# The last unit of a MoE encoder: adding the residual in the output banks with TensorE, and the last chunk's products ahead of the scatters

## The chip, the cores and the metric

One core of a Trainium2 chip runs the whole kernel. The metric is the device time of one execution in microseconds (us), as the median of several runs.

## What is computed

One encoder layer on 256 tokens of width 1024, all in fp32: a mixer with attention in two head groups, and then the part that matters here, a mixture of experts, followed by the last norm:

```python
h = h + mix @ w_o[l]
h = h + hier_moe(rms_norm(h, norm2_g[l]), ...)      # 32 experts, top-2 of one group of 8
return rms_norm(h, final_g)
# an expert: (silu(x @ w_gate) * (x @ w_up) * combine) @ w_down,  w_gate and w_up 1024x512, w_down 512x1024
```

Every expert's weights (6 MB) are read from HBM, 32 experts, so about 200 MB in all. At the end stands h plus the experts' sum, normalised by the root of its mean square and multiplied with final_g.

## The kernel before

The program is written by hand, engine by engine, with semaphores; nothing is scheduled for it. The tokens lie in two tiles of 128 (t = 0, 1), and each tile's 1024 columns in two halves of 512. The columns of h are kept permuted: the tile holds 8 blocks of 128 columns (`h_cols`, each block contiguous), and `h_rows` is the same memory read so that 8 elements in succession lie 128 elements (512 bytes) apart.

```python
h_cols = h.rearrange("p t (c k) -> p t c k", c=KC)
h_rows = h.rearrange("p t (c k) -> p t k c", c=KC)
```

The experts are worked through in ten units (`UNITS`) of two or four experts (`WAYS`); the last three have four. A unit gathers its tokens (L1266), multiplies with gate and up (`products`, L1304), takes silu times up on DVE (L963), transposes that on TensorE (`turn_act`, L1316), copies it back to SBUF on DVE (`hT_out`, L958), multiplies with down (`down_chunk`, L1322), copies the result out on ACT (`down_out`, L670, into `y_slots`) and scatters it onto the tokens with one matmul per tile and half (`scatter`, L1355). The scatters of all units accumulate in the four banks Y0 to Y3 (bank Y0 + 2t + half), which stay open through the whole mixture. Unit i's scatter is issued two units later, behind the gate products; in the last unit, i = 9, both scatter(7) and scatter(8) stand between the gate and the up products.

Weights come through a ring of 12 slots of 2 MB, issued by SP in the order of use; each load waits until the products that used the slot are done. The last unit's down weights come in four pieces (`LAST_PIECES`, L427): chunks 0 and 1, chunk 2, the first half of chunk 3, its second half. TensorE multiplies them as they land (`last_products(0)` to `(3)`), with the spreading of final_g over the partitions between them (L1448, eight matmuls, copied out by ACT, L668). `last_scatter(k)` (L1442) adds one tile and half in the order `LAST_ORDER` = (0,0), (1,0), (0,1), (1,1).

After each of the four last scatters DVE adds h to the bank into `h_sum` in SBUF (L1026), reading `h_rows`. ACT squares each sum with an accumulator (L694). POOL multiplies tile 0's first half with final_g (L523), DVE tile 1's (L1058). DVE adds the two sums of squares of a tile (L1057, L1060), POOL raises to the power -0.5 (L526), DVE scales the second halves (L1063) and ACT the first (L699), and three DMAs write the output (L443, L445, L701).

A float32 matmul stands in the trace as two passes, each with its own load of the stationary operand, and four experts of 32 rows each run side by side in the array: 16 such matmuls are 32 rows of the trace, in 8 groups of four.

Of the kernel before, what the change touches and what calls it, by code (L numbers as in the profile page):

```python
# [10 lines left out]
ALU = mybir.AluOpType  # L11
# [4 lines left out]
D = 1024  # L16
# [101 lines left out]
def build_encoder(nc, x, x_cols, gain_cols, norm1_g, w_in, qn_g, kn_g, sink, rel_bias, gnorm_a, gnorm_b, w_o, norm2_g,  # L118
# [11 lines left out]
    with ExitStack() as ctx:  # L130
# [108 lines left out]
        def scratch(n):  # L239
# [52 lines left out]
            sem, ("down_done", "y_ready", "place_ready", "scattered", "summed"))  # L292
        ov_turned, ov_nT, ov_free, ov_in, ov_gu, ov_silu, ov_act, ov_act_turned, ov_hT, ov_y, ov_added = map(
# [155 lines left out]
        def _(pool):  # L449
# [71 lines left out]
            pool.wait_ge(final_g_cut, 1)  # L521
            pool.wait_ge(ssf_ready, 1)
            pool.tensor_tensor(final_out[:, 0, 0:512], h_sum[:, 0, 0:512], final_gb[:, 0:512], ALU.mult).then_inc(gained_t0, 1)  # L523
# [5 lines left out]
        def _(act):  # L529
# [154 lines left out]
            with act.If(over > 0):  # L684
# [4 lines left out]
                act.wait_ge(ov_added, TT * EXPERTS)  # L689
# [14 lines left out]
        def _(dve):  # L704
# [319 lines left out]
            for k, (t, half) in enumerate(LAST_ORDER):  # L1024
                dve.wait_ge(scattered, 4 * UNITS + k + 1)
                dve.tensor_tensor(h_sum[:, t, 512 * half:512 * half + 512].rearrange("p (k c) -> p k c", c=KC), h_rows[:, t, 64 * half:64 * half + 64, :],  # L1026
                                  ps[Y0 + 2 * t + half][:].rearrange("p (k c) -> p k c", c=KC), ALU.add).then_inc(summed, 1)

            over = dve.value_load(over_flag[0:1, 0:1], min_val=0, max_val=1)
            with dve.If(over > 0):  # L1030
                ov_nT_sb = slots[3].rearrange("p (c t) -> p c t", c=16)
                link(dve.tensor_tensor(weight_over, weight_over, bcast(rstd2, 2, EXPERTS), ALU.mult))
# [496 lines left out]
```

## Time and profile before

| what | value |
|---|---|
| median of 3 runs | 568.03 us (567.9 to 568.98) |
| the profiled execution, its own time | 568.0 us |
| span from first to last instruction in it | 565.7 us, so 2.3 us lie around it |
| PE busy, DVE busy, ACT busy | 80%, 20%, 12% of the span |
| DMA | 217.67 MB at a mean of 385 GB/s |
| mean granted TensorE clock | 0.904 of full speed |

The profile has a page with shares of busy time, a chain of work followed back from the last instruction, and groups of instructions. The trace behind it gives single instructions in order of time: start, duration, engine, line of the kernel, operation, output and inputs, how often in a row, and in brackets how long the engine had been idle before it and what ended that. `x8` after a matmul counts passes.

### The profile page before, as it was taken

Reading aid. Unit: us, or ns where it says so; the run is one execution under the profiler, and the core shown is the slowest. Engines: PE = TensorE matmul, PEld = TensorE weight load, DVE = VectorE, ACT = ScalarE, POOL = GpSimd, SP = SyncE. Lnnn points to the kernel's source line nnn. Section 1 sums busy time; section 2 is a strip of 40 time slices with the busy share of each in tenths; the row PEclk is TensorE's granted clock in tenths of the full one; section 3 lists DMA queues with packets and bytes.
Section 4 is the critical chain, followed back from the end, with each engine's and each line's share of the span. In section 5 each row is a group of like instructions: output and inputs, shape, how many; then the busy total and the mean of one; then the engine's idle time right before and its main releaser. Section 6 shows DMA issues by size and latency. Waiting matters only on the chain.

```text
span 565.7 us, 6390 instructions
## 1 busy us (share of the span) xinstructions
PE 452.3 (80%) x2562; PEld 204.1 (36%) x2562; DVE 111.4 (20%) x353; ACT 67.9 (12%) x160; POOL 23.6 (4%) x53
## 2 busy tenths in 40 slices
PE   9999999989999996478999936952776385557884
PEld 3456776474535342132353401410223021312231
DVE  1017764262112030030110300300021001200004
ACT  1125332121010100100101001000100000000104
POOL 0232200100000000000000000000000000000001
PEclk9999999999999998797999968877977787876988
DMA  8989991947999999999999999999999999999981
GB/s 305 382 333 429 425 367 29 416 151 232 410 392 422 428 426 425 429 431 427 423 426 430 430 426 427 426 426 426 426 432 432 425 427 426 426 426 427 423 342 76
DMA packets 27390, 217.67 MB, mean 385 GB/s; under 512 B 5433, under 2 KB 6713, under 8 KB 14561
## 3 DMA queue, kind: packets, MB, share of 16 engines
q1 hardware_dynamic: 23120, 215.09, 91.5%
q10 hardware_dynamic: 4240, 2.17, 1.4%
q8 instruction: 21, 0.34, 0.2%
q14 instruction: 9, 0.07, 0.0%
HBM read 216.18 MB, written 1.06 MB: 384 GB/s over the span
## 4 chain that ended last, share of the span: by engine, by line
PE 48%; DMA 46%; DVE 2%; SPq 1%; issue 1%; DVEq 0%; POOL 0%; ACT 0%
DMA ring<-in_w_down_dram 32%; PE bank L1304 10%; PE bank L1322 10%; DMA ring<-in_w_gate_dram 8%; PE bank L1083 7%; DMA ring<-in_w_up_dram 6%; PE bank L1155 5%; PE bank L1266 3%; PE bank L1145 2%; PE bank L1123 1%; PE bank L1355 1%; PE bank L1368 1%; PE bank L1070 1%; PE bank L1075 1%; PE bank L1134 1%; SPq L327 1%
## 5 line engine op out<-in xcount | busy, mean ns | idle before, releaser
L1304 PE MATMUL bank<-ring,region_x 128*32 128x512 f32 (+1 forms) x992 | 155.3, 679 | 74.2 <-DMA ring<-in_w_gate_dram 45.4
L1304 PEld LDWEIGHTS bank<-ring,region_x 128*32 128x32 f32 (+1 forms) x992 | 44.8, 128 | 176.0 <-issue 176.0
L1322 PE MATMUL bank<-ring,region_q 128*32 128x512 f32 (+1 forms) x512 | 82.8, 692 | 26.0 <-DMA ring<-in_w_down_dram 24.3
L969 DVE COPY region_q<-bank 128x256 f32<-128x256 f32 x10 | 4.2, 424 | 318.3 <-PE bank L1284 318.3
L1322 PEld LDWEIGHTS bank<-ring,region_q 128*32 128x32 f32 (+1 forms) x512 | 24.0, 131 | 75.9 <-issue 74.0
L1083 PE MATMUL bank<-ring,region_x 128*128 128x512 f32 x96 | 42.5, 595 | 0.0
L670 ACT ACTIVATE region_x<-bank 128x512 f32<-128x512 f32 x20 | 11.1, 595 | 254.7 <-PE bank L1355 241.1
L1266 PE MATMUL bank<-region_q,h 128*128 128x128 f32 x320 | 40.1, 279 | 0.8 <-DVE region_q L937 0.8
L1266 PEld LDWEIGHTS bank<-region_q,h 128*128 128x128 f32 x320 | 37.4, 192 | 9.2 <-issue 8.2
L1355 PE MATMUL bank<-region_x,region_q 128*128 128x512 f32 x72 | 33.3, 605 | 1.2 <-ACT region_x L670 1.2
L1155 PE MATMUL bank<-ring,region_q 128*128 128x512 f32 x64 | 28.9, 597 | 0.0
L1083 PEld LDWEIGHTS bank<-ring,region_x 128*128 128x128 f32 x96 | 17.8, 190 | 21.7 <-issue 21.6
L651 ACT ACTIVATE region_x<-bank,gT 128x128 f32<-128x128 f32 x40 | 11.4, 368 | 115.5 <-PE bank L1266 115.5
L1355 PEld LDWEIGHTS bank<-region_x,region_q 128*128 128x128 f32 x72 | 12.9, 189 | 21.6 <-issue 19.6
L523 POOL TENSOR_TENSOR ring<-ring 128x512 f32<-128x512 f32 x1 | 1.3, 1272 | 441.0 <-ACT region_q L694 441.0
L1155 PEld LDWEIGHTS bank<-ring,region_q 128*128 128x128 f32 x64 | 11.6, 190 | 12.6 <-issue 12.6
L1145 PE MATMUL bank<-ring 128*128 128x65 f32 x128 | 15.2, 272 | 0.0
L1145 PEld LDWEIGHTS bank<-ring 128*128 128x128 f32 x128 | 15.0, 192 | 0.5 <-issue 0.5
L946 DVE TENSOR_SCALAR region_q<-cst,sorted_rw 128x32 f32<-128x32 f32 (+1 forms) x56 | 12.4, 298 | 0.0
L937 DVE TENSOR_SCALAR region_q<-cst,sorted_rw,stat 128x32 f32<-128x32 f32 (+1 forms) x56 | 12.4, 297 | 0.0
L783 DVE SCALAR_TENSOR_TENSOR h<-bank,stat,h 128x512 f32<-128x512 f32 x8 | 6.0, 751 | 20.6 <-PE bank L1155 17.8
L958 DVE COPY region_q<-bank 128x512 f32<-128x512 f32 x10 | 6.9, 692 | 15.9 <-PE bank L1316 15.9
(188 smaller groups left out, 262.7 us busy)
## 6 DMA issues: line engine op xcount, KB each, us to landing
ring<-in_w_gate_dram SPq DMA_DIRECT2D x28, 2048.0 KB, 39.2
ring<-in_w_up_dram SPq DMA_DIRECT2D x28, 2048.0 KB, 38.8
ring<-in_w_down_dram SPq DMA_DIRECT2D x24, 2048.0 KB, 39.3
ring<-in_w_down_dram SPq DMA_DIRECT2D x12, 1024.0 KB, 14.2
ring<-in_w_in_dram SPq DMA_DIRECT2D x8, 512.0 KB, 8.5
ring<-in_w_o_dram SPq DMA_DIRECT2D x2, 2048.0 KB, 12.2
ring<-in_w_gate_dram SPq DMA_DIRECT2D x8, 512.0 KB, 6.5
ring<-in_w_gate_dram SPq DMA_DIRECT2D x4, 1024.0 KB, 8.2
```

Of the source, the lines that this page charges most:

```text
L651: last = act.activation(xgT[:, c, :], ps[GD0][:, c * P:(c + 1) * P], ACT.Copy, scale=g2_rows[:, c:c + 1])
L670: act.activation(y_slots[:, 512 * half:512 * half + 512], ps[GD0 + half][:], ACT.Copy).then_inc(y_ready, 1)
L937: last = dve.tensor_scalar(pick[:, t, rows * a:rows * (a + 1)], iota1[:, 0:rows], ranks[:, t, e0 + a:e0 + a + 1], rstd2[:, t:t + 1], ALU.i ...
L946: last = dve.tensor_scalar(pick_w[:, t, rows * a:rows * (a + 1)], iota1[:, 0:rows], ranks[:, t, e0 + a:e0 + a + 1], weights[:, t, e0 + a:e ...
L958: dve.tensor_copy(hT, ps[GATE][:].rearrange("p (c s) -> p c s", c=FC)).then_inc(hT_ready, 1)
L1083: return pe.matmul(ps[bank][:], xT[:, c, t * P:(t + 1) * P], cols, start=(c == 0), stop=(c == KC - 1))
L1145: last = pe.matmul(ps[6][:, 65 * l:65 * l + 65], probsT[:, s % 2, kt, l, :], v_sb[:, kt, 2 * g + l // 2, :], start=(kt == 0), stop=(kt == ...
L1155: last = pe.matmul(ps[bank][:], mixT[:, 1 - g, t, c - 4 * g, :], w_o_sb[g][:, c - 4 * g, 512 * half:512 * half + 512], start=(c == 4 * g), ...
L1266: last = pe.matmul(ps[GD0 + b][:, c * P:(c + 1) * P], h_cols[:, t, 4 * b + c, :], pick[:, t, :], start=(t == 0), stop=(t == TT - 1))
L1304: last = pe.matmul(ps[bank][rows, :], xgT[:, c, rows], slots[fill_slot(f + a)][:, c * F:(c + 1) * F], start=(c == 0), stop=(c == KC - 1))
L1322: last = pe.matmul(ps[GD0 + half][rows, :], hT[:, c, rows], slots[fill_slot(f + a)][:, c * D + 512 * half:c * D + 512 * half + 512], start ...
L1355: last = pe.matmul(ps[Y0 + k][:], place_w[i % 2][:, (k // 2) * P:(k // 2 + 1) * P], y_slots[:, 512 * (k % 2):512 * (k % 2) + 512], start=( ...
```

## The change

TensorE now adds h itself: in the last unit, behind scatter(8) and ahead of the up products, four matmuls with the identity as the stationary operand and `h_rows` as the moving one accumulate h into Y0 to Y3 (`add_h`). DVE's four additions are gone, and all that read `h_sum` reads the banks: ACT's squares, the multiplications with final_g (both on DVE now; POOL's is gone) and the final scaling. The squares run in the order (0,0), (0,1), (1,0), (1,1), and tile 1's first waits until DVE has read its bank (`gained_t1`). DVE computes tile 1's mean behind tile 0's final scaling. ACT copies both halves of the spread final_g ahead of both halves of y. On TensorE, last_products(3) now stands ahead of last_scatter(0). The branch for an overflow of an expert's capacity, which is not taken with these inputs, copies the banks out and back.

```diff
@@ gpsimd
-            pool.wait_ge(final_g_cut, 1)
-            pool.wait_ge(ssf_ready, 1)
-            pool.tensor_tensor(final_out[:, 0, 0:512], h_sum[:, 0, 0:512], final_gb[:, 0:512], ALU.mult).then_inc(gained_t0, 1)
@@ scalar, down_out
                 act.wait_ge(scattered, 4 * i + 4)
-                for half in range(2):
-                    if i == UNITS - 1:
+                if i == UNITS - 1:
+                    for half in range(2):
                         act.wait_ge(final_g_turned, half + 1)
                         act.activation(final_gb[:, 512 * half:512 * half + 512], ps[(UP, GATE)[half]][:], ACT.Copy).then_inc(final_g_cut, 1)
+                for half in range(2):
                     act.wait_ge(down_done, 2 * i + 1 + half)
                     act.activation(y_slots[:, 512 * half:512 * half + 512], ps[GD0 + half][:], ACT.Copy).then_inc(y_ready, 1)
@@ scalar, tail
-            for k, (t, half) in enumerate(LAST_ORDER):
-                act.wait_ge(summed, k + 1)
-                if k:
-                    act.wait_ge(ssf_ready, k)
-                act.activation(silu_sb, h_sum[:, t, 512 * half:512 * half + 512], ACT.Square, scale=D ** -0.5,
+            for n, (t, half) in enumerate(((0, 0), (0, 1), (1, 0), (1, 1))):
+                act.wait_ge(scattered, 4 * UNITS + LAST_ORDER.index((t, half)) + 1)
+                if n:
+                    act.wait_ge(ssf_ready, n)
+                if (t, half) == (1, 0):
+                    act.wait_ge(gained_t1, 1)
+                act.activation(silu_sb, ps[Y0 + 2 * t + half][:], ACT.Square, scale=D ** -0.5,
                                accum_out=ssf[:, 2 * t + half:2 * t + half + 1]).then_inc(ssf_ready, 1)
@@ vector, tail
-            for k, (t, half) in enumerate(LAST_ORDER):
-                dve.wait_ge(scattered, 4 * UNITS + k + 1)
-                dve.tensor_tensor(h_sum[:, t, 512 * half:512 * half + 512].rearrange("p (k c) -> p k c", c=KC), h_rows[:, t, 64 * half:64 * half + 64, :],
-                                  ps[Y0 + 2 * t + half][:].rearrange("p (k c) -> p k c", c=KC), ALU.add).then_inc(summed, 1)
...
+            def mean(t):
+                dve.scalar_tensor_tensor(rstdf[:, t:t + 1], ssf[:, 2 * t:2 * t + 1], EPS, ssf[:, 2 * t + 1:2 * t + 2],
+                                         ALU.add, ALU.add).then_inc(mean_ready, 1)
+
+            dve.wait_ge(scattered, 4 * UNITS + 2)
             dve.wait_ge(final_g_cut, 2)
-            dve.wait_ge(ssf_ready, 3)
-            dve.scalar_tensor_tensor(rstdf[:, 0:1], ssf[:, 0:1], EPS, ssf[:, 1:2], ALU.add, ALU.add).then_inc(mean_ready, 1)
-            dve.tensor_tensor(final_out[:, 1, 0:512], h_sum[:, 1, 0:512], final_gb[:, 0:512], ALU.mult).then_inc(gained_t1, 1)
-            dve.wait_ge(ssf_ready, 4)
-            dve.scalar_tensor_tensor(rstdf[:, 1:2], ssf[:, 2:3], EPS, ssf[:, 3:4], ALU.add, ALU.add).then_inc(mean_ready, 1)
+            dve.tensor_tensor(final_out[:, 1, 0:512], ps[Y2][:], final_gb[:, 0:512], ALU.mult).then_inc(gained_t1, 1)
+            dve.wait_ge(ssf_ready, 1)
+            dve.tensor_tensor(final_out[:, 0, 0:512], ps[Y0][:], final_gb[:, 0:512], ALU.mult).then_inc(gained_t0, 1)
+            dve.wait_ge(ssf_ready, 2)
+            mean(0)
             for t in range(TT):
+                if t:
+                    dve.wait_ge(ssf_ready, 4)
+                    mean(1)
                 dve.wait_ge(rstdf_ready, t + 1)
-                dve.scalar_tensor_tensor(final_out[:, t, 512:1024], h_sum[:, t, 512:1024], rstdf[:, t:t + 1], final_gb[:, 512:1024],
+                dve.scalar_tensor_tensor(final_out[:, t, 512:1024], ps[Y1 + 2 * t][:], rstdf[:, t:t + 1], final_gb[:, 512:1024],
                                          ALU.mult, ALU.mult).then_inc(out_ready, 1)
@@ tensor
+            def add_h():
+                for t in range(TT):
+                    for half in range(2):
+                        pe.matmul(ps[Y0 + 2 * t + half][:], ident, h_rows[:, t, 64 * half:64 * half + 64, :], start=False, stop=False)
@@ tensor, the loop over units
                 if i == UNITS - 1:
                     scatter(i - 1)
+                    add_h()
@@ tensor, tail
             last_products(2)
+            last_products(3)
             last_scatter(0)
-            last_products(3)
             last_scatter(1)
```

How the instructions stand on TensorE from the last unit's gate products to the last scatter (a matmul of L1322 or L1304 is one expert's; L1316 transposes the activations, L1448 spreads final_g). Before:

```order
L1304 MATMUL bank<-ring,region_x 32x512 x32
L1355 MATMUL bank<-region_x,region_q 128x512 x8
L1304 MATMUL bank<-ring,region_x 32x512 x16
L1284 MATMUL bank<-cst,region_q 128x128 x2
L1304 MATMUL bank<-ring,region_x 32x512 x16
L1316 MATMUL bank<-cst,region_q 128x128 x4
L1322 MATMUL bank<-ring,region_q 32x512 x16
L1448 MATMUL bank<-cst,gT 128x128 x4
L1322 MATMUL bank<-ring,region_q 32x512 x8
L1448 MATMUL bank<-cst,gT 128x128 x4
L1322 MATMUL bank<-ring,region_q 32x512 x4
L1442 MATMUL bank<-region_x,region_q 128x512
L1322 MATMUL bank<-ring,region_q 32x512 x4
L1442 MATMUL bank<-region_x,region_q 128x512 x3
```

The same stretch in the changed kernel:

```order
L1316 MATMUL bank<-ring,region_x 32x512 x32
L1367 MATMUL bank<-region_x,region_q 128x512 x8
L1375 MATMUL bank<-h,cst 128x512 x4
L1316 MATMUL bank<-ring,region_x 32x512 x16
L1296 MATMUL bank<-cst,region_q 128x128 x2
L1316 MATMUL bank<-ring,region_x 32x512 x16
L1328 MATMUL bank<-cst,region_q 128x128 x4
L1334 MATMUL bank<-ring,region_q 32x512 x16
L1466 MATMUL bank<-cst,gT 128x128 x4
L1334 MATMUL bank<-ring,region_q 32x512 x8
L1466 MATMUL bank<-cst,gT 128x128 x4
L1334 MATMUL bank<-ring,region_q 32x512 x8
L1460 MATMUL bank<-region_x,region_q 128x512 x4
```

Four matmuls of 512 columns that read h stand new ahead of the up products, and the last four products are joined to the four ahead of them, with all four scatters behind.

DVE at the end, with what each instruction waits for, before (the overflow branch left out between the two pieces):

```order
L1026 TENSOR_TENSOR ring<-h,bank 128x512 [waits scattered] x4
```

```order
L1057 SCALAR_TENSOR_TENSOR stat<-stat 128x1 [waits ssf_ready,final_g_cut]
L1058 TENSOR_TENSOR ring<-ring 128x512
L1060 SCALAR_TENSOR_TENSOR stat<-stat 128x1 [waits ssf_ready]
L1063 SCALAR_TENSOR_TENSOR ring<-ring,stat 128x512 [waits rstdf_ready] x2
```

and in the changed kernel:

```order
L1065 TENSOR_TENSOR ring<-bank,ring 128x512 [waits final_g_cut,scattered]
L1067 TENSOR_TENSOR ring<-bank,ring 128x512 [waits ssf_ready]
L1060 SCALAR_TENSOR_TENSOR stat<-stat 128x1 [waits ssf_ready]
L1075 SCALAR_TENSOR_TENSOR ring<-bank,stat,ring 128x512 [waits rstdf_ready]
L1060 SCALAR_TENSOR_TENSOR stat<-stat 128x1 [waits ssf_ready]
L1075 SCALAR_TENSOR_TENSOR ring<-bank,stat,ring 128x512 [waits rstdf_ready]
```

The four additions are gone, a multiplication has come from POOL, and the second mean stands behind the first final scaling.

## Rows read from the trace of the kernel before

**Rows 1.** The page, busy tenths in 40 slices of the span: TensorE and DMA.

```profile
PE   9999999989999996478999936952776385557884
...
DMA  8989991947999999999999999999999999999981
```

**Rows 2.** The chain that ended last, in order of time, two pieces (start us, us, what).

```profile
503.84 38.22 DMA ring<-in_w_down_dram
...
556.35 2.02 DVE ring L1026 x2
```

**Rows 3.** The timeline of TensorE's matmuls in the last unit, from scatter(8) on.

```profile
527.01 3.70 PE L1355 MATMUL bank<-region_x,region_q 128*128 128x512 f32 x8 [1.18 <-ACT region_x L670]
531.88 3.64 PE L1304 MATMUL bank<-ring,region_x 128*32 128x512 f32 x32 [1.17 <-DMA ring<-in_w_up_dram]
...
540.34 0.75 PE L1316 MATMUL bank<-cst,region_q 128*128 128x128 f32 x4 [0.88 <-DVE region_q L963]
542.19 5.20 PE L1322 MATMUL bank<-ring,region_q 128*32 128x512 f32 x32 [1.11 <-DMA ring<-in_w_down_dram]
...
551.35 1.06 PE L1322 MATMUL bank<-ring,region_q 128*32 128x512 f32 x8
553.13 1.13 PE L1442 MATMUL bank<-region_x,region_q 128*128 128x512 f32 x2 [0.72 <-ACT region_x L670]
554.19 1.07 PE L1322 MATMUL bank<-ring,region_q 128*32 128x512 f32 x8
555.18 2.84 PE L1442 MATMUL bank<-region_x,region_q 128*128 128x512 f32 x6
```

**Rows 4.** Groups by line and form: count, busy us, mean ns of one.

```profile
L963 DVE TENSOR_TENSOR region_q<-region_q,bank 128x512 f32<-128x512 f32 x10 | 6.9, 688 | 11.8 <-PE bank L1304 11.8
...
L1316 PEld LDWEIGHTS bank<-cst,region_q 128*128 128x128 f32 x40 | 5.6, 206 | 1.8 <-DVE region_q L963 1.8
...
L1026 DVE TENSOR_TENSOR ring<-h,bank 128x512 f32<-128x512 f32 x4 | 4.0, 1056 | 13.4 <-PE bank L1442 13.4
...
L1284 PEld LDWEIGHTS bank<-cst,region_q 128*128 128x128 f32 x20 | 2.1, 141 | 7.5 <-issue 7.5
```

**Rows 5.** Windows: busy of PE, PEld, DVE, ACT, POOL; clock, DMA share, GB/s.

```profile
542.00:545.40 3.40, 3.21 (x16) 0.91 (x20) 0.00 (x0) 0.00 (x0) 0.00 (x0) 0.50 1.02 396
545.40:548.80 3.40, 3.40 (x32) 1.53 (x28) 0.00 (x0) 0.23 (x1) 0.00 (x0) 1.00 0.98 364
```

**Rows 6.** Line L427, its last DMA: duration of the issue, start, time to landing.

```profile
L427 SPq DMA_DIRECT2D ring<-in_w_down_dram x1: 937/937/937, 542.6 to 542.6; - x1
...
DMA to landing us min/median/max: 9.8/9.8/9.8
```

**Rows 7.** The timeline of DVE, ACT and POOL at the end, one engine after another.

```profile
541.12 0.69 DVE L958 COPY region_q<-bank 128x512 f32<-128x512 f32 x1 [0.84 <-PE bank L1316]
...
556.35 2.96 DVE L1026 TENSOR_TENSOR ring<-h,bank 128x512 f32<-128x512 f32 x3 [0.97 <-PE bank L1442]
559.26 0.16 DVE L1057 SCALAR_TENSOR_TENSOR stat<-stat 128x1 f32<-128x1 f32 x1
...
560.46 1.41 DVE L1063 SCALAR_TENSOR_TENSOR ring<-ring,stat 128x512 f32<-128x512 f32 x2 [0.20 <-POOL stat L526]
...
552.48 0.60 ACT L670 ACTIVATE region_x<-bank 128x512 f32<-128x512 f32 x1 [3.31 <-PE bank L1322]
...
556.30 0.63 ACT L694 ACTIVATE region_q<-ring 128x512 f32<-128x512 f32 x1 [0.39 <-issue]
556.84 0.19 ACT L694 ACTIVATION_READ_ACCUMULATOR region_q<-ring 128x1 f32 x1
...
559.50 1.43 POOL L526 TENSOR_TENSOR stat<-stat 128x1 f32<-128x1 f32 x2 [1.06 <-DVE stat L1057]
```

**Rows 8.** DMA issues of the output: KB, us from issue to landing.

```profile
out_dram<-ring SPq DMA_DIRECT2D x1, 512.0 KB, 2.7
...
out_dram<-ring SPq DMA_DIRECT2D x1, 256.0 KB, 3.5
```

More of the change, by code:

```diff
@@ L292, in build_encoder @@
             sem, ("down_done", "y_ready", "place_ready", "scattered", "summed"))
+        restored = sem("restored")
         ov_turned, ov_nT, ov_free, ov_in, ov_gu, ov_silu, ov_act, ov_act_turned, ov_hT, ov_y, ov_added = map(
@@ L688, in _ @@
                         act.activation(silu_sb, ps[0][:], ACT.Silu, scale=rstd2[:, t:t + 1]).then_inc(ov_silu, 1)
-                act.wait_ge(ov_added, TT * EXPERTS)
-            for k, (t, half) in enumerate(LAST_ORDER):
-                act.wait_ge(summed, k + 1)
-                if k:
-                    act.wait_ge(ssf_ready, k)
-                act.activation(silu_sb, h_sum[:, t, 512 * half:512 * half + 512], ACT.Square, scale=D ** -0.5,
+                act.wait_ge(restored, 4)
+            for n, (t, half) in enumerate(((0, 0), (0, 1), (1, 0), (1, 1))):
[5 more added lines that the diff above has]
+                act.activation(silu_sb, ps[Y0 + 2 * t + half][:], ACT.Square, scale=D ** -0.5,
                                accum_out=ssf[:, 2 * t + half:2 * t + half + 1]).then_inc(ssf_ready, 1)
@@ L1031, in _ @@
                 ov_nT_sb = slots[3].rearrange("p (c t) -> p c t", c=16)
+                dve.wait_ge(scattered, 4 * UNITS + 4)
+                for t in range(TT):
+                    for half in range(2):
+                        dve.tensor_copy(h_sum[:, t, 512 * half:512 * half + 512], ps[Y0 + 2 * t + half][:]).then_inc(summed, 1)
                 link(dve.tensor_tensor(weight_over, weight_over, bcast(rstd2, 2, EXPERTS), ALU.mult))
@@ L1053, in _ @@
                 dve.wait_ge(ov_added, TT * EXPERTS)
-            dve.wait_ge(final_g_cut, 2)
-            dve.wait_ge(ssf_ready, 3)
-            dve.scalar_tensor_tensor(rstdf[:, 0:1], ssf[:, 0:1], EPS, ssf[:, 1:2], ALU.add, ALU.add).then_inc(mean_ready, 1)
-            dve.tensor_tensor(final_out[:, 1, 0:512], h_sum[:, 1, 0:512], final_gb[:, 0:512], ALU.mult).then_inc(gained_t1, 1)
-            dve.wait_ge(ssf_ready, 4)
-            dve.scalar_tensor_tensor(rstdf[:, 1:2], ssf[:, 2:3], EPS, ssf[:, 3:4], ALU.add, ALU.add).then_inc(mean_ready, 1)
+                for t in range(TT):
+                    for half in range(2):
+                        dve.tensor_copy(ps[Y0 + 2 * t + half][:], h_sum[:, t, 512 * half:512 * half + 512]).then_inc(restored, 1)
+                dve.wait_ge(restored, 4)
+            def mean(t):
+                dve.scalar_tensor_tensor(rstdf[:, t:t + 1], ssf[:, 2 * t:2 * t + 1], EPS, ssf[:, 2 * t + 1:2 * t + 2],
+                                         ALU.add, ALU.add).then_inc(mean_ready, 1)
+            dve.wait_ge(scattered, 4 * UNITS + 2)
+            dve.wait_ge(final_g_cut, 2)
+            dve.tensor_tensor(final_out[:, 1, 0:512], ps[Y2][:], final_gb[:, 0:512], ALU.mult).then_inc(gained_t1, 1)
[3 more added lines that the diff above has]
+            mean(0)
             for t in range(TT):
+                if t:
+                    dve.wait_ge(ssf_ready, 4)
+                    mean(1)
                 dve.wait_ge(rstdf_ready, t + 1)
-                dve.scalar_tensor_tensor(final_out[:, t, 512:1024], h_sum[:, t, 512:1024], rstdf[:, t:t + 1], final_gb[:, 512:1024],
+                dve.scalar_tensor_tensor(final_out[:, t, 512:1024], ps[Y1 + 2 * t][:], rstdf[:, t:t + 1], final_gb[:, 512:1024],
                                          ALU.mult, ALU.mult).then_inc(out_ready, 1)
@@ L1358, in scatter @@
                 return last
+            def add_h():
+                for t in range(TT):
+                    for half in range(2):
+                        pe.matmul(ps[Y0 + 2 * t + half][:], ident, h_rows[:, t, 64 * half:64 * half + 64, :], start=False, stop=False)
             def first_gate(chunks):
```

## Prediction

> **What bounds the kernel now.** I read the slices of the page first. DMA is at nine tenths or more in every slice from the eleventh to the 38th of 40, TensorE is not [rows 1]: through the mixture the stream of weights sets the pace, and TensorE waits for it. The chain of waits says the same up to 542 us: one stretch of 38.2 us is the first piece of the last down weights on its way [rows 2]. So time can be gained or lost only in what follows the stream. From the timeline of TensorE the reader is to see where that begins. The up products start at 531.88 after 1.17 us of waiting for their weights. The last down products start at 542.19, and there the wait for the weights is nearly over: the activations' copy on DVE had ended at 541.81 [rows 7], and where TensorE waits for such a copy alone it starts 0.05 us after its end (ACT's copy ends at 553.08 [rows 7], the scatter starts at 553.13 [rows 3]). It could have started at 541.86, so DMA holds it up by **0.33 us** and no more. From then on TensorE has no wait for DMA: the last piece lands at 542.6 + 9.8 = 552.4 [rows 6], and its products start at 554.19 [rows 3]. The end is a chain TensorE, ACT, TensorE, DVE, POOL, DVE, output DMA. What delays TensorE's handing over at 540 us by more than 0.33 us delays the end; what shortens the chain behind 551 us brings it forward.
>
> **add_h, the new work.** Four float32 matmuls are 8 passes. The last scatters give the full rate: 2 passes take 1.13 us and 6 take 2.84, so four more cost 1.71 us, 0.4275 each, and 0.28 us are the pipeline's end, which the next matmul does not wait for [rows 3]. The 8 passes of scatter(8) take 3.70 us, again 8 x 0.4275 + 0.28, so the array is free for add_h at 527.01 + 3.42 = 530.43. The up products wait until 531.88. The cover is thus 1.45 us. 8 passes at full rate take 3.42 us: 1.97 us over the cover.
>
> But the moving operand is h_rows, whose successive elements lie 512 bytes apart, and no row of the trace shows a matmul that streams such an operand. Two rows show what such reading costs other readers. DVE's addition of h (L1026) reads the same h_rows and takes 1056 ns, while DVE's product of a bank and a contiguous SBUF tile of the same size takes 688 ns: 368 ns more for 512 elements, 0.72 ns each. TensorE's own load of 128 columns for a transpose takes 141 ns when they are contiguous (L1284) and 206 ns when they lie 16 bytes apart (L1316): 0.51 ns more each, 1.61 ns in all per column [rows 4]. A pass at full rate takes 0.4275 us / 512 = 0.83 ns per column. The bounds for a pass:
> - below, 0.43 us: nothing is lost, 3.42 us for add_h;
> - the extra of the load row, 0.83 + 0.51 ns per column: 0.69 us, 5.5 us for add_h;
> - the load's whole time per column, 1.61 ns: 0.82 us, 6.6 us;
> - above, DVE's time per element with its fixed part in, 1056 ns / 512 = 2.06 ns: 1.06 us, 8.4 us.
>
> I take 6.6 us, since it is TensorE's own reading, and what a reader can fetch per element is more likely a limit that takes the place of the 0.83 ns than something added to it.
>
> The Trainium skill, page "SBUF — State Buffer", section "Door 1: The DMA port swizzle", says that SBUF is read in lines of 16 bytes, that full speed needs at least two hits in a line, and that each access that crosses to a new line pays. By that rule every element of h_rows pays, so it speaks against this change; it names no price. By it the sum is somewhere above the 567.8 us that the 3.42 us give (below); without it the 567.8 stand. The rows of DVE and of the load agree with it, in their 1056 and 206 ns; that a matmul's moving operand pays too no row here shows.
>
> With 6.6 us the array is free at 537.05, and the up products start 5.17 us later than now. Queued behind them are the transposes, DVE's two copies, the down products, everything to the end: **+5.17 us**. SP's queue is not touched: the last down weights go into slots that unit 8 freed at 502, so the stream stays where it is and all pieces land by 552.4, before they are wanted (piece 0 at 542.06, wanted at about 547). The 0.33 us of waiting goes: **-0.33 us**.
>
> **The order of the last products.** After products(2) start at 551.35, eight passes take 0.86 us, so products(3) could start at 552.2 and end their passes at 553.06. In front of the first scatter, ACT's copy of the first half ends at 553.08 as now, so that scatter still starts at 553.13. The other three follow at 553.98, 554.84 and 555.69, the second half's copy being done at about 553.95. Now the last one starts at 555.18 + 4 x 0.43 = 556.89. TensorE gains 1.2 us. In the changed kernel products(3) come later by the shift above, so the landing at 552.4 never holds them up.
>
> **DVE's additions.** The first addition starts 1.16 us after its scatter (553.13 to 554.29), so I take a bank as readable 1.16 us after its scatter starts. Now the additions end at 559.31 [rows 7], and all that follows hangs on them. I lay the new chain out without the shift. Banks are readable at 554.29 (0,0), 555.14 (1,0), 556.00 (0,1), 556.85 (1,1). A square takes 0.73 us to the end of its accumulator's read [rows 7]. The square of (0,1) runs from 556.04 to 556.77; DVE's two multiplications, 0.69 us each, run from 555.17 to 556.56 and so lie beside it. Tile 0's mean follows at 556.87. From the mean to the final scaling by way of POOL are 560.46 - 559.26 = 1.20 us [rows 7]: scaling from 558.07 to 558.82. ACT's squares of tile 1, 0.9 us apart with the issue between them, end at 558.6, before DVE is free for the second mean at 558.85, which the new order puts there: it costs another 1.20 us, so the second scaling starts at 560.05 and ends at 560.80. Now it ends at 561.87. The removed additions and the earlier scatters bring tile 0's scaling forward from 560.46 to 558.07 and the last square from 559.34 to about 557.9, and the second trip over POOL gives some of it back: **-1.07 us**.
>
> **The output.** Now all of it is issued within 0.6 us, and the last 256 KB land 3.5 us after their issue, behind the others. Tile 0 will be issued about 1.4 us before tile 1, so that tile 1's 512 KB go alone, as the first 512 KB do now in 2.7 us [rows 8]: **-0.8 us** (bounds 0 and -0.8, as the 256 KB beside it may still collide).
>
> The moved copy of final_g on ACT and POOL's removed multiplication cost and save nothing: the copy starts at 551.5, when ACT is idle until 552.48.
>
> **Sum.** 5.17 - 0.33 - 1.07 - 0.8 = +3.0 us. The profiled execution took 568.0 us (span 565.7 and 2.3 around it), the median is 568.03: **571.0 us**. With the 5.5 us for add_h it is 569.9, with 8.4 us 572.8.
>
> **Rivals.**
> *TensorE streams h_rows at full rate.* Then the shift is 1.97 - 0.33 = 1.64 us, against 1.87 us of gain: -0.2 us, **567.8**, no change. For it: nothing in the trace shows a matmul slowed by its moving operand, and the array takes a float32 column in 0.83 ns, slower than it might read. Against it: rows 4.
> *The clock stays high at the last handing over.* Now the down products run at 0.50 of full speed from 542.0 to 545.4 and at 1.00 from there [rows 5], after TensorE had stood idle for 0.88 and 1.11 us around its transposes [rows 3]; their 32 passes take 5.20 us where 8 x 0.4275 = 3.42 are needed, which costs 1.78 us. With the wait for DMA gone the second gap is 0.33 us shorter, and add_h fills the gap before. If the 1.2 GHz stretch does not come, 1.78 us are gained: **566.0** with the full rate, faster than before, **569.2** with the slow reading. This is the rival on the other side; with the clock kept the kernel is faster by over 1.1 us if add_h takes less than 4.3 us (4.3 - 1.45 - 0.33 - 1.87 - 1.78 = -1.1). Against it: the gaps shrink little, from 1.99 to 1.66 us.
> *A second stretch at half clock.* While h_rows is read slowly, the array works at half its rate; if the clock falls there as well, the up products lose the same 1.78 us: **572.8**.
>
> **How the numbers follow.** Slow reading with the clock as now 0.47 (569.9 to 571.5), slow reading with the clock kept 0.13, a second low stretch 0.08, full rate 0.22, full rate with the clock kept 0.10. A measurement of this kernel tells 0.2%, 1.1 us, from no change. Faster than 566.9 is the last case and the edge of the one before: 0.13. Within 0.2% are the rest of the full rate and a part of the slow reading with the clock kept: 0.25. Slower: 0.62. The range leaves out most of the fastest case and the top of the slowest: 567.2 to 572.4; the likeliest case alone spans 569.9 to 571.5.
>
> **What would show it.** Right: 8 passes of the line of add_h spaced by 0.7 us or more, up products starting at about 537, no wait for DMA ahead of the last down products, and from the start of products(2) to the last final scaling 9.5 us in place of 10.5. Wrong: passes 0.43 us apart, up products at 533.9, or a clock of 1.00 all through the last down products.

## The result and the profile after

The changed kernel takes **570.04 us** (median of 20 runs, 567.96 to 573.43) against 568.07 of the kernel before on the same chip (20 runs, 566.59 to 570.03): ratio **1.0035**, 95% interval [1.0023, 1.0048], slower by 2.0 us. Forecast were 571.0 us, slower. The profiled execution took 568.67 us (span 566.6), so it is one of the faster ones, and it must not be set against the median term by term.

TensorE's matmuls in the last unit, from the gate products on (the timeline, engine PE; the columns are start, duration, what, and the idle time before):

```profile
513.22 8.44 PE L1316 MATMUL bank<-ring,region_x 128*32 128x512 f32 x64 [9.83 <-DMA ring<-in_w_gate_dram]
...
526.47 3.70 PE L1367 MATMUL bank<-region_x,region_q 128*128 128x512 f32 x8 [1.18 <-ACT region_x L669]
530.01 7.09 PE L1375 MATMUL bank<-h,cst 128*128 128x512 f32 x8
537.03 3.64 PE L1316 MATMUL bank<-ring,region_x 128*32 128x512 f32 x32
...
547.02 3.64 PE L1334 MATMUL bank<-ring,region_q 128*32 128x512 f32 x32 [0.78 <-DVE region_q L959]
...
554.62 1.92 PE L1334 MATMUL bank<-ring,region_q 128*32 128x512 f32 x16
556.48 3.70 PE L1460 MATMUL bank<-region_x,region_q 128*128 128x512 f32 x8
```

These answer to [rows 3]. add_h (L1375) takes 7.09 us, 0.88 us for each of its 8 passes, where the scatter ahead of it takes 3.70 for as many. The up products no longer wait for their weights: they start 10.56 us after the start of scatter(8), before 4.87. The wait for the down weights is gone too (0.78 us behind DVE). And the first down products take 3.64 us, not 5.20: this execution kept the clock at 1.00 there. It was 1.00 in the rows of add_h too (530.01 to 537.03).

The tail, DVE and POOL from their timelines, answering to [rows 7]:

```profile
558.50 0.69 DVE L1065 TENSOR_TENSOR ring<-bank,ring 128x512 f32<-128x512 f32 x1 [11.53 <-PE bank L1460]
559.11 0.68 DVE L1067 TENSOR_TENSOR ring<-bank,ring 128x512 f32<-128x512 f32 x1
560.08 0.16 DVE L1060 SCALAR_TENSOR_TENSOR stat<-stat 128x1 f32<-128x1 f32 x1 [0.29 <-ACT region_q L695]
560.89 0.75 DVE L1075 SCALAR_TENSOR_TENSOR ring<-bank,stat,ring 128x512 f32<-128x512 f32 x1 [0.65 <-POOL stat L524]
561.63 0.16 DVE L1060 SCALAR_TENSOR_TENSOR stat<-stat 128x1 f32<-128x1 f32 x1
562.44 0.75 DVE L1075 SCALAR_TENSOR_TENSOR ring<-bank,stat,ring 128x512 f32<-128x512 f32 x1 [0.66 <-POOL stat L524]
...
560.32 0.54 POOL L524 TENSOR_TENSOR stat<-stat 128x1 f32<-128x1 f32 x1 [444.50 <-DVE stat L1060]
```

From the start of products(2), 554.62, to the end of the last scaling, 563.19, are **8.57 us**; before, 551.35 to 561.87, 10.52. From the mean to the scaling by way of POOL are 0.81 us, not 1.20. ACT, between its first square and its second, waits 1.03 us for the third scatter:

```profile
557.64 0.60 ACT L695 ACTIVATE region_q<-bank 128x512 f32<-128x512 f32 x1 [0.43 <-PE bank L1460]
...
559.36 0.60 ACT L695 ACTIVATE region_q<-bank 128x512 f32<-128x512 f32 x1 [1.03 <-PE bank L1460]
```

The two spans differ by 0.9 us, and the starts and ends above give where: the gate products start 0.94 later, since their weights came later, and from there scatter(8) comes 1.48 sooner, since they ran longer at the high clock (8.44 us against 9.93), so scatter(8) starts 0.54 earlier in all; from there to the up products +5.69; from those to the down products 9.99 against 10.31, -0.32; from there to products(2) 7.60 against 9.16, -1.56 (the clock); the tail -1.95; from the last scaling to the end of the span 3.45 against 3.87, -0.4. The sum is +0.9.

### The profile page after: what moved, and what is told of

Its sections match the earlier page's. It is cut to its first block and busy times, and to the rows that moved or that the text cites. A ratio compares the mean times of both kernels' runs of the same rounds, so it can differ in the third digit from the quotient of the medians.

```text
span 566.6 us, 6401 instructions
## 1 busy us (share of the span) xinstructions
PE 455.5 (80%) x2570; PEld 206.9 (37%) x2570; DVE 108.1 (19%) x350; ACT 67.9 (12%) x160; POOL 22.0 (4%) x52
## 3 DMA queue, kind: packets, MB, share of 16 engines
HBM read 216.18 MB, written 1.06 MB: 383 GB/s over the span
## 5 line engine op out<-in xcount | busy, mean ns | idle before, releaser
L1316 PE MATMUL bank<-ring,region_x 128*32 128x512 f32 (+1 forms) x992 | 153.7, 672 | 74.5 <-DMA ring<-in_w_gate_dram 45.9
L1316 PEld LDWEIGHTS bank<-ring,region_x 128*32 128x32 f32 (+1 forms) x992 | 45.1, 128 | 175.3 <-issue 175.3
L1334 PE MATMUL bank<-ring,region_q 128*32 128x512 f32 (+1 forms) x512 | 80.2, 672 | 24.9 <-DMA ring<-in_w_down_dram 22.4
L1278 PE MATMUL bank<-region_q,h 128*128 128x128 f32 x320 | 41.6, 285 | 0.8 <-DVE region_q L938 0.8
L1278 PEld LDWEIGHTS bank<-region_q,h 128*128 128x128 f32 x320 | 38.9, 199 | 9.2 <-issue 8.2
L1367 PEld LDWEIGHTS bank<-region_x,region_q 128*128 128x128 f32 x72 | 12.9, 189 | 21.6 <-issue 19.6
```

The costliest lines, as they stand in the source:

```text
L1278: last = pe.matmul(ps[GD0 + b][:, c * P:(c + 1) * P], h_cols[:, t, 4 * b + c, :], pick[:, t, :], start=(t == 0), stop=(t == TT - 1))
L1316: last = pe.matmul(ps[bank][rows, :], xgT[:, c, rows], slots[fill_slot(f + a)][:, c * F:(c + 1) * F], start=(c == 0), stop=(c == KC - 1))
L1334: last = pe.matmul(ps[GD0 + half][rows, :], hT[:, c, rows], slots[fill_slot(f + a)][:, c * D + 512 * half:c * D + 512 * half + 512], start ...
L1367: last = pe.matmul(ps[Y0 + k][:], place_w[i % 2][:, (k // 2) * P:(k // 2 + 1) * P], y_slots[:, 512 * (k % 2):512 * (k % 2) + 512], start=( ...
```

## The experiments

They ran on three chips, each beside the kernel before: e1 to e4 on the first, where its median was 568.12 us, m1 and e5 to e7 on the second (568.43), e8 to e10 on the third (568.06), 29 runs each. All ratios are to it.

**e1: contiguous reading in the same place.**

```diff
-                        pe.matmul(ps[Y0 + 2 * t + half][:], ident, h_rows[:, t, 64 * half:64 * half + 64, :], start=False, stop=False)
+                        pe.matmul(ps[Y0 + 2 * t + half][:], ident, h[:, t, 512 * half:512 * half + 512], start=False, stop=False)
```

> add_h reads 512 contiguous elements of h in place of h_rows, so each half gets its columns in the wrong order; number, size, place and banks of its four matmuls are as in the change. Theory (slow reading): in the changed kernel add_h's 8 passes take 7.09 us, because successive elements lie 512 bytes apart; contiguous they take 8 x 0.4275 + 0.28 = 3.7 us, the up products start 3.6 us earlier after scatter(8), and the median falls from 570.0 to about 566.4 with the wait for the first down piece at 0 to 0.1 us. Rival (the passes are slow for another reason, such as accumulating into banks or the identity's load): they stay at 7.1 us and the time at 570.0.

Measured: 566.74 us (10 runs), ratio 0.9976 [0.9957, 0.9994]. The timeline of TensorE:

```profile
529.27 3.60 PE L1375 MATMUL bank<-h,cst 128*128 128x512 f32 x8
532.80 3.64 PE L1316 MATMUL bank<-ring,region_x 128*32 128x512 f32 x32
...
542.79 5.34 PE L1334 MATMUL bank<-ring,region_q 128*32 128x512 f32 x32 [0.79 <-DVE region_q L959]
```

The passes cost half. Only the step of the moving operand was changed, so the slow reading is the cost of add_h, 3.5 us of its 7.09, and it alone turns a change that would be faster than before into one that is slower. The last row is the low clock at the last down products: it came here as in the kernel before.

**m1: which step costs.** Eight matmuls stand in add_h's place, so the sums in the banks are not the layer's (`flat` is h as 2048 columns in succession):

```diff
+                by2 = flat.rearrange("p (n s) -> p n s", s=2)
+                by3 = flat[:, 0:1536].rearrange("p (n s) -> p n s", s=3)
+                by4 = flat.rearrange("p (n s) -> p n s", s=4)
+                by8 = flat.rearrange("p (n s) -> p n s", s=8)
+                pe.matmul(ps[Y0][:], ident, flat[:, 0:512], start=False, stop=False)
+                pe.matmul(ps[Y1][:], ident, by2[:, 0:512, 0], start=False, stop=False)
+                pe.matmul(ps[Y2][:], ident, by3[:, 0:512, 0], start=False, stop=False)
+                pe.matmul(ps[Y3][:], ident, by4[:, 0:512, 0], start=False, stop=False)
+                pe.matmul(ps[Y0][:], ident, by4[:, 0:256, 0:2], start=False, stop=False)
+                pe.matmul(ps[Y1][:], ident, by8[:, 0:128, 0:4], start=False, stop=False)
+                pe.matmul(ps[Y2][:], ident, h_rows[:, 0, 0:64, :], start=False, stop=False)
+                pe.matmul(ps[Y3][:], ident, flat[:, 512:1024], start=False, stop=False)
```

> In add_h's place in the changed kernel stand eight matmuls of 512 columns into the four banks, each with another moving operand out of h, so the output is not the layer's: contiguous; every 2nd, every 3rd, every 4th element; 2 of every 4; 4 of every 8; h_rows; contiguous. Measured is the time of a pass, 0.43 us contiguous and 0.88 us for h_rows in the changed kernel. Theory A (a read per 16-byte line, at least two hits in it for full speed): every 2nd and both groups stay at 0.43, every 4th costs 0.88 as h_rows does, every 3rd lies between or at 0.88. Theory B (any step but one costs the same): every 2nd and every 3rd take 0.88 too. Theory C (the long distance of 512 bytes costs, not the line): every 4th stays near 0.43 and h_rows alone costs 0.88.

Measured, in the order of the diff (timeline of TensorE; each row is one matmul of two passes):

```profile
530.23 1.02 PE L1378 MATMUL bank<-h,cst 128*128 128x512 f32 x2
531.09 1.06 PE L1379 MATMUL bank<-h,cst 128*128 128x512 f32 x2
531.99 1.51 PE L1380 MATMUL bank<-h,cst 128*128 128x512 f32 x2
533.33 1.97 PE L1381 MATMUL bank<-h,cst 128*128 128x512 f32 x2
535.12 1.08 PE L1382 MATMUL bank<-h,cst 128*128 128x512 f32 x2
536.05 1.02 PE L1383 MATMUL bank<-h,cst 128*128 128x512 f32 x2
536.90 1.89 PE L1384 MATMUL bank<-h,cst 128*128 128x512 f32 x2
538.61 1.04 PE L1385 MATMUL bank<-h,cst 128*128 128x512 f32 x2
```

From start to start: contiguous 0.86 us, every 2nd element 0.90, every 3rd 1.34, every 4th 1.79, 2 of every 4 0.93, 4 of every 8 0.85, h_rows 1.71. Theory A stands in all seven. A step of 16 bytes costs about as much as one of 512, so it is not the distance, and what counts is whether elements that follow each other share 16 bytes. The prices go with the number of 16-byte pieces that are read, as an estimate from these rows: every 4th element is a piece of its own, 1.79 us; of every 3rd, four elements lie in three pieces, and 3/4 of 1.79 is 1.34; of every 2nd, two share a piece, and half is 0.90; contiguous elements would come to 0.45, and there the 0.86 us of the full rate are the limit. With no two in one piece a float32 matmul of 512 columns costs about twice the contiguous one, 1.71 or 1.79 us against 0.86. The Trainium skill, page "SBUF — State Buffer", section "Door 1: The DMA port swizzle", says that full speed needs at least two hits in a line of 16 bytes and that each access to a new line pays; these rows agree with it for TensorE's moving operand. The single run's 571.23 us says nothing more.

**e2: add_h where TensorE waits anyway**, ahead of the last unit's gate products.

```diff
+                if i == UNITS - 1:
+                    add_h()
                 if i == 1:
                     products(i, ways(i), fill_at(i, 0, 0), GATE, gate_done, gate_pieces, KC // 2)
...
                     scatter(i - 1)
-                    add_h()
```

> add_h moved ahead of the last unit's gate products, where TensorE waited 9.8 us for weights in the changed kernel; its reading is unchanged. Theory (the place is the cost): add_h still takes 7.1 us but nothing of it delays the gate products, the up products start again about 5 us after scatter(8)'s start after waiting for their weights, the last down products wait for their first piece as before, and only the shorter tail is left: 568.1 - 1.95 - 0.5 = 565.6 us, between 565 and 567 with the clock at the last handing over as in the kernel before or better. Rival (reading h slowly disturbs more than TensorE, by way of SBUF or the clock): passes or gate products get longer there and the time stays above 567.5.

Measured: **566.39 us** (12 runs), ratio 0.9975 [0.9963, 0.9988]. The timeline of TensorE:

```profile
502.18 7.16 PE L1375 MATMUL bank<-h,cst 128*128 128x512 f32 x8
513.13 9.37 PE L1316 MATMUL bank<-ring,region_x 128*32 128x512 f32 x64 [3.80 <-DMA ring<-in_w_gate_dram]
...
532.72 3.64 PE L1316 MATMUL bank<-ring,region_x 128*32 128x512 f32 x32 [1.70 <-DMA ring<-in_w_up_dram]
...
552.85 1.06 PE L1334 MATMUL bank<-ring,region_q 128*32 128x512 f32 x8 [1.13 <-DMA ring<-in_w_down_dram]
```

add_h is as slow as before and costs nothing: 3.80 us of waiting are left behind it. The place is worth 3.65 us (570.04 to 566.39, not run side by side; 3.4 us by the two ratios). The rival, a disturbance by the slow reading, does not show: the gate products take 9.37 us, within the 8.4 to 9.95 us of the other profiles. A new limit shows in the last row: TensorE now waits 1.13 us for the last piece of the down weights. The expected 565.6 counted on none.

**e3: only the order of the last products undone** in the changed kernel.

```diff
-            last_products(3)
             last_scatter(0)
+            last_products(3)
             last_scatter(1)
```

> The changed kernel with last_products(3) put back behind last_scatter(0). Theory (the order of the last products is worth something now that DVE's additions are gone): the last three scatters start 1.2 us later, tile 1's chain with them, but tile 0's too, since its second half is the third scatter: start of products(2) to the last final scaling grows from 9.4 to about 10.3 us, median 570.9. Rival (the squares on ACT and the two trips over POOL bound the end, not TensorE): under 0.3 us of difference, 570.0 to 570.3.

Measured: 571.29 us (4 runs), ratio 1.0079 [1.0051, 1.0107]. From the start of products(2), 553.72, to the end of the last scaling, 563.41, are 9.69 us against 8.57. By the profiles the order is worth 1.1 us in the changed kernel, as the theory has it (the 9.4 us in the expectation was the forecast's figure, not the profile's). The median says the same less sharply, 1.25 us from four runs that lie between 568.9 and 574.0.

**e4: only the order of the last products** in the kernel before (the same lines the other way round).

> The kernel before with last_products(3) ahead of last_scatter(0) and nothing else. Theory (DVE's additions of 1.05 us each bound the tail): the four additions run back to back from 554.3 on that profile's clock and end at about 558.4 in place of 559.3, since the second no longer waits for its scatter: -0.9 us, 567.2. Rival (TensorE bounds the tail): the full 1.2 us, 566.9; or nothing, if the squares and POOL's product of 1.27 us set it: 568.1.

Measured: 568.42 us (10 runs), ratio 1.0009 [0.9993, 1.0025]: no gain. Yet the mechanism is in the profile. The timeline of DVE:

```profile
555.84 3.92 DVE L1026 TENSOR_TENSOR ring<-h,bank 128x512 f32<-128x512 f32 x4 [10.71 <-PE bank L1442]
```

The additions run back to back, and from products(2), 552.78, to the last scaling's end, 562.29, are 9.51 us against 10.52. My reading is that this gain holds only where TensorE comes late: where it comes early, products(3) wait for the last piece (1.13 us in e2) and now hold the first scatter back. That was not tested for this kernel, and in e10, where TensorE came early, products(3) behind the first scatter gained nothing either. The profiled time, 568.43 against 568.0 us, does not show the tail's 1.0 us: its gate weights came 1.63 us later than in the profile of before.

**e5: e2 with e3's order.** The diffs are those two.

> add_h ahead of the gate products as in e2, and last_products(3) back behind last_scatter(0). In e2's profile TensorE waited 1.13 us for the last piece of the down weights ahead of products(3). Theory (the order of the last products helps where TensorE comes late and hurts where the last piece does): the first scatter now runs in that wait, the other three start 0.86 us earlier, time 566.4 - 0.8 = 565.6 us as long as the clock stays high at the last handing over. Rival (TensorE's order decides as in e3): slower by 0.9, 567.2.

Measured: 566.47 us (12 runs), ratio 0.9968 [0.9954, 0.9982], the same as e2. In its profile the clock had fallen at the last down products (5.34 us), TensorE came late and no wait for the last piece showed; but that execution, 568.14 us, was the slowest of the twelve. Neither theory was right about the median.

**e6: e2 with the squares in the scatters' order and both means first.**

```diff
-            for n, (t, half) in enumerate(((0, 0), (0, 1), (1, 0), (1, 1))):
+            for n, (t, half) in enumerate(LAST_ORDER):
...
             dve.wait_ge(final_g_cut, 2)
-            dve.tensor_tensor(final_out[:, 1, 0:512], ps[Y2][:], final_gb[:, 0:512], ALU.mult).then_inc(gained_t1, 1)
             dve.wait_ge(ssf_ready, 1)
             dve.tensor_tensor(final_out[:, 0, 0:512], ps[Y0][:], final_gb[:, 0:512], ALU.mult).then_inc(gained_t0, 1)
             dve.wait_ge(ssf_ready, 2)
+            dve.tensor_tensor(final_out[:, 1, 0:512], ps[Y2][:], final_gb[:, 0:512], ALU.mult).then_inc(gained_t1, 1)
+            dve.wait_ge(ssf_ready, 3)
             mean(0)
+            dve.wait_ge(ssf_ready, 4)
+            mean(1)
             for t in range(TT):
-                if t:
-                    dve.wait_ge(ssf_ready, 4)
-                    mean(1)
```

> As e2, with ACT's squares in the order of the scatters again, (0,0), (1,0), (0,1), (1,1), DVE's product for tile 0 ahead of tile 1's, and both means ahead of the final scalings. Theory (in the changed kernel the end hangs on ACT, which waits 1.03 us for the third scatter after its first square, and on a second trip over POOL behind the first scaling): the last square ends 0.6 us earlier, the two scalings of 0.75 us follow each other, and from products(3) to the last scaling's end it is 0.5 to 0.6 us shorter: 565.8 us. Rival (the output DMAs then collide again as in the kernel before and give it back): 566.3.

Measured: **565.48 us** (12 runs), ratio **0.9961** [0.9942, 0.9979], the fastest version. Its products(2) start at 551.67, and the timeline of DVE ends with

```profile
557.13 0.16 DVE L1058 SCALAR_TENSOR_TENSOR stat<-stat 128x1 f32<-128x1 f32 x1 [0.17 <-ACT region_q L693]
557.99 0.16 DVE L1058 SCALAR_TENSOR_TENSOR stat<-stat 128x1 f32<-128x1 f32 x1 [0.70 <-ACT region_q L693]
558.06 1.49 DVE L1072 SCALAR_TENSOR_TENSOR ring<-bank,stat,ring 128x512 f32<-128x512 f32 x2
```

so the tail is 7.88 us in place of 8.57 in the changed kernel, and from products(3) it is 7.02 against 7.71 in e2. ACT's wait for the third scatter is gone, and the second trip over POOL runs beside the first scaling. The rival holds in part: the outputs are issued 0.67 us apart, not 0.99, and from the last scaling to the end of the span are 3.80 us, 3.46 in e2, so 0.34 of the 0.7 us are given back. The profiles thus show 0.35 us of gain over e2; the medians' 0.9 is more than that, on two chips and with intervals that overlap, and against e7 on its own chip it is 0.86.

**e7: e2 with the gaps filled** around the last transposes.

```diff
+            def fill():
+                pe.matmul(ps[GD0][:, 0:448], ident, cst[:, 0:448], start=True, stop=True)
+
+            fill()
             turn_act(UNITS - 1)
+            fill()
```

> As e2, with one matmul of 448 constant columns into a free bank ahead of the last transposes and one behind them, in gaps of TensorE of 0.88 and 0.78 us. Theory (part of the executions lose up to 1.7 us because TensorE's clock falls to 1.2 GHz at the last handing over, others don't, and that is much of the spread): the passes lie in the gaps and delay nothing, the clock stays at 1.00 through the last down products in the profile, and the median falls by up to 0.5 us, the upper end of the runs most. Rival (the clock at this place does not matter, since the last piece of the weights lands late anyway): 566.2 to 566.5, unchanged.

Measured: 566.34 us (12 runs), ratio 0.9966 [0.9952, 0.9981], as e2. The clock stayed at 1.00 and TensorE waited 1.12 us for the last piece. Since e2's profile had the clock at 1.00 without the filling, this profile cannot show that the filling keeps it there; the median agrees with the rival.

**e8: the changed kernel again. e9: the changed kernel with e7's filling.**

> The changed kernel once more, unedited, for a second profile and for comparison with e9 on the same chip. Expected 570.0 us. If the clock at the last handing over differs from execution to execution, this profile may show 0.50 during the first down products (5.2 us for their 32 passes) where the first showed 1.00 (3.64 us), with a time about 1.7 us longer.

> The changed kernel with e7's two matmuls of constants around the last transposes, add_h left at its place. Here TensorE, not the last piece of the weights, bounds the tail. Theory (the clock falls at the last handing over in a part of the executions and costs up to 1.78 us there): the median falls below e8's by 0.4 to 1.2 us and the highest times go. Rival (the spread comes from elsewhere, such as the clock at the gate products or the stream): the same as e8 within 0.3 us.

Measured: e8 570.30 us (12 runs), ratio 1.0039 [1.0017, 1.0060]; e9 569.40 (12 runs), 1.0028 [1.0008, 1.0047]. The difference is of the expected size, but the intervals overlap, and the highest time fell only from 573.4 to 571.6: not shown. Both profiles have the last down products at full clock, as the first profile of the changed kernel and e3's had without filling, so e8's expected 0.50 there did not come and there was nothing for the filling to save; e9's profiled execution is 2.0 us shorter because its gate weights came 1.06 us earlier and its gate products took 1.05 us less. e8's profile shows another thing, on the timeline of TensorE and in a window (busy of PE, PEld, DVE, ACT, POOL; clock, DMA share, GB/s):

```profile
512.90 9.95 PE L1316 MATMUL bank<-ring,region_x 128*32 128x512 f32 x64 [10.03 <-DMA ring<-in_w_gate_dram]
...
538.19 3.64 PE L1316 MATMUL bank<-ring,region_x 128*32 128x512 f32 x32
```

```profile
512.90:518.50 5.60, 5.60 (x28) 1.54 (x32) 0.00 (x0) 0.00 (x0) 0.00 (x0) 0.50 1.02 430
```

Its gate products took 9.95 us, because the clock was at 0.50 for 5.6 us of them, and the up products came 25.29 us after the gate products' start. In the first profile of the same kernel they took 8.44 us and the distance is 23.81 us: all 1.5 us arrive at the up products. In the kernel before and in e4, which has its gate and up products unchanged, they do not:

```profile
512.28 9.93 PE L1304 MATMUL bank<-ring,region_x 128*32 128x512 f32 x64 [10.05 <-DMA ring<-in_w_gate_dram]
```

is followed there by a wait of 1.17 us for the up weights [rows 3], and e4's timeline has

```profile
513.91 8.40 PE L1304 MATMUL bank<-ring,region_x 128*32 128x512 f32 x64 [9.88 <-DMA ring<-in_w_gate_dram]
...
533.49 5.34 PE L1304 MATMUL bank<-ring,region_x 128*32 128x512 f32 x32 [2.67 <-DMA ring<-in_w_up_dram]
```

1.53 us faster, and 1.50 us more of waiting. All profiles with nothing or with h_rows in that place say it (us; the distance is from the start of the gate products to the start of the up products):

| profile | gate products | distance | wait for the up weights |
|---|---|---|---|
| e6, add_h early | 8.39 | 19.57 | 2.68 |
| e4, no add_h | 8.40 | 19.58 | 2.67 |
| e10, add_h early | 8.99 | 19.61 | 2.11 |
| e7, add_h early | 9.21 | 19.61 | 1.90 |
| e2, add_h early | 9.37 | 19.59 | 1.70 |
| before | 9.93 | 19.60 | 1.17 |
| e5, add_h early | 9.94 | 19.59 | 1.14 |
| changed, first profile | 8.44 | 23.81 | none |
| e3 | 8.45 | 23.79 | none |
| e9 | 8.90 | 24.24 | none |
| e8 | 9.95 | 25.29 | none |

Where nothing stands between scatter(8) and the up products, the weights set the distance, 19.6 us, whatever the clock did. With add_h there it is the gate products and 15.34 to 15.37 us. So add_h at its place does not only use up the wait, it puts the clock at the gate products on the path, and its cost differs by that clock: 4.2 us at 8.44, 5.7 us at 9.95.

**e10: all together**, e6 with e7's filling and e3's order.

> add_h early (e2), squares in scatter order and both means first (e6), the two matmuls of constants (e7) and last_products(3) behind last_scatter(0) (e5). Theory: with the clock held high TensorE always comes before the last piece, and then the first scatter fits into that wait, 0.8 us less than e6 less what DVE and ACT need: 565.0 us. Rival: the order of the products gives nothing once ACT's squares bound the end, or the clock falls elsewhere: 565.5 as e6.

Measured: 567.12 us (12 runs), ratio 0.9977 [0.9959, 0.9995], not better than e6. On its timeline the first scatter waits 0.72 us for ACT, as in [rows 3], and delays products(3). Counted from the start of the gate products, the last scaling ends after 47.11 us, in e6 after 46.74: the order does not gain there, it costs 0.4 us, so the rival was nearer than the theory. Why the median is 1.6 us over e6's stays open; the chips differ, the intervals overlap, and its gate weights came at 514.11 in the profile, e6's at 512.81. That arrival, which nothing changed here acts on, lies between 511.84 and 514.11 over all the profiles.

## Why the prediction was right

**add_h.** The step that decided, slow reading of h_rows, was right, and e1 and m1 show its cause. The size was near: 6.6 us by the load's time per column, measured 7.02 us (530.01 to 537.03), within the bounds of 3.4 to 8.4. A pass takes 0.88 us, 1.71 ns per element; the load row's 1.61 was near, and reading it as a limit in place of the full rate, not as an addition to it (5.5 us), was the right choice: in m1 every 2nd element needs half as many pieces as every 4th and costs 0.90 us, hardly more than contiguous, so the greater of the two limits counts and not their sum. The rival of the full rate falls, though e1 shows what it would have given: 566.7 against the 567.8 worked out. The rival of a second stretch at half clock falls too: the clock was 1.00 through add_h, and the up products took 3.64 us.

**The cover.** Taken as 1.45 us from one profile, whose gate products took 9.93 us. For the same length of gate products that is right: e8, with 9.95, has 25.29 us to the up products against 19.60, +5.69 against the forecast's 5.17, 0.4 of it add_h's size. But the cover is a different number in each execution, 1.17 us of waiting in one and 2.67 in another, and in the first profile of the changed kernel, with 8.44, the shift is only +4.21. The forecast missed this: it looked for the clock only at the last handing over.

**The last wait for DMA.** -0.33 forecast, -0.32 measured.

**The tail.** -1.07 forecast, -1.95 measured, from products(2) to the last scaling: 8.57 us where 9.5 were expected. The step that failed is the price of a trip over POOL, the "another 1.20 us" and the one before it: it takes 0.81. In the trace of before POOL's two powers took 919 and 537 ns, and the mean hid that:

```profile
L526 POOL TENSOR_TENSOR stat<-stat x2: 537/728/919, 559.5 to 560.4; 128x1 f32<-128x1 f32 x2
```

The long one started while DVE was multiplying two SBUF tiles:

```profile
559.34 0.69 DVE L1058 TENSOR_TENSOR ring<-ring 128x512 f32<-128x512 f32 x1
```

e4, which has the same end, shows 919 and 539 again. In the changed kernel DVE is idle then, and both take 0.54:

```profile
L524 POOL TENSOR_TENSOR stat<-stat x2: 538/540/543, 560.3 to 561.9; 128x1 f32<-128x1 f32 x2
```

Twice 0.39 us is 0.8 of the missing 0.9. That DVE's multiplication is what slowed POOL is read from the overlap; no run varied it alone.

**The output.** -0.8 forecast, about -0.4 measured: the issues are 1.0 us apart, not 1.4, since the second trip over POOL is 0.39 us shorter, and ACT's 256 KB land after 3.0 us, not 2.7.

**The clock.** Here the likeliest case was not what the profiles show. It had the low stretch at the last down products, as in the profile of before, and a clock of 1.00 all through them was named as a sign of being wrong. The stretch came there in before, e1 and e5, and not in the changed kernel's two profiles, e2, e3, e4, e6 and m1; e4 and e6 had it at the up products. So the mechanism in both profiles of the changed kernel is that of the rival, slow reading with the clock kept, and the likeliest case's band, 569.9 to 571.5, holds the median of 570.04 in part by luck. The price of the stretch was also too high: 1.78 us came from 5.20, which has the pipeline's end in it, less 3.42, which has not; the up products' 3.64 in [rows 3] give 1.56, and 1.56 is what the profiles show. With it the rival's 569.2 becomes 569.4.

The fair pair is before and e8, whose gate products took the same time. Counted from their start to the end of the span, e8 is 1.5 us longer: +5.69 - 0.32 - 1.95 - 0.4 = +3.0, less 1.56 for the clock. The +3.0 is the forecast's own sum, in which three errors cancel (+0.5, -0.9, +0.4), so its closeness is luck as well. The medians differ by 2.0. Which share of the executions of either kernel has which stretch of low clock is not known, and e9 did not settle it. The rival "clock kept, full rate", 566.0, is near e1's 566.7 in number only, since e1's profile had the low stretch; there the tail and the output brought 0.5 us more than the forecast gave them.

## What to carry to other kernels

Before work is moved to TensorE, look at the moving operand: with float32, successive elements none of which share 16 bytes doubled the time of each matmul, at a distance of 16 bytes as at 512. Work that is not urgent belongs in the longest wait of the engine, not in the last one: the same 7 us cost 3.65 us at the place chosen and nothing 28 us earlier, in a wait of 10 us. A short wait for DMA behind other work is also a buffer against that work's varying clock, so look at more than one profile before spending it.

## What was not expected of the hardware

- POOL's power on a [128, 1] operand takes 537 to 543 ns, and 919 where DVE's multiplication of two SBUF tiles was already running when it started (before and e4). The second power of before started just ahead of DVE's scaling of two SBUF tiles (L1063) and took 537, and e6's second started while DVE scaled a bank with one SBUF tile and took 0.54 us. No run tested it alone.
- A moving operand with every 3rd float32 takes 0.67 us per pass of 512 columns, between 0.43 (contiguous) and 0.90 (every 4th); every 2nd costs 0.45 (m1).
- The same kernel's gate products take 8.44 or 9.95 us in two profiles: after a wait of 9.8 and 10.0 us the clock stayed at 0.50 for about 2.6 us of them in one and 5.6 in the other.
